# Seven half products for pairs of gate slots in the last FFN of a two-layer decoder step

## The reference, cut to what matters

```python
def swiglu(x, w_gate, w_up, w_down):
    h = jax.nn.silu(jnp.einsum('bsd,df->bsf', x, w_gate)) * jnp.einsum('bsd,df->bsf', x, w_up)
    return jnp.einsum('bsf,fd->bsd', h, w_down)
...
    x = x + rms_norm(swiglu(h, w_ffn_gate[i], w_ffn_up[i], w_ffn_down[i]), g_post_ffn[i])
```

## Time and profile before

| | |
|---|---|
| median of 3 runs | 2570.3 us (2569.86 to 2570.42) |
| span of the profiled execution | 2568.3 us |
| the profiled execution's own time | not listed beside its span; the median is 2.0 us over the span |
| PE / DVE / ACT busy | 2555.7 / 1501.2 / 1011.8 us |
| mean granted clock of PE | 0.999 |

### The profile page before, as it was taken

One profiled execution on the slowest core, in us unless ns is written; L12 is line 12 of the kernel. 1 busy time (PEld: TensorE's weight loads), 2 busy tenths in 40 slices (PEclk: granted clock), 3 DMA queues, 4 the chain that ended last, 5 costly groups with the idle time before them and its releaser, 6 DMA issues.

```text
span 2568.3 us, 40710 instructions
## 1 busy us (share of the span) xinstructions
PE 2555.7 (100%) x17201; PEld 2315.5 (90%) x17201; DVE 1501.2 (58%) x2320; ACT 1011.8 (39%) x1452; POOL 0.2 (0%) x4
## 2 busy tenths in 40 slices
PE   9999999999999999999999999999999999999998
PEld 7899898887988998899999988998887989999998
DVE  6644575666466673357854775328876486434435
ACT  5443355452344443345434444335552343222222
POOL 0000000000000000000000000000000000000000
PEclk9999999999999999999999999999999999999999
DMA  6454445445433433553333343444346334322222
GB/s 226 136 184 154 138 159 159 140 119 163 148 113 107 135 100 97 169 161 95 112 108 103 103 147 117 139 147 127 108 130 202 115 115 139 104 83 85 87 84 91
DMA packets 176704, 330.38 MB, mean 129 GB/s; under 512 B 19964, under 2 KB 93436, under 8 KB 176524
## 3 DMA queue, kind: packets, MB, share of 16 engines
q1 hardware_dynamic: 176524, 327.79, 40.9%
HBM read 271.46 MB, written 56.28 MB: 128 GB/s over the span
## 4 chain that ended last, share of the span: by engine, by line
PE 93%; DVE 4%; ACT 2%; issue 1%; DMA 0%; SPq 0%; ACTq 0%; DVEq 0%
PE ps L1016 81%; PE ps L1030 3%; PE ps L1342 1%; PE ps L1284 1%; PE ps L1428 1%; DVE Y L1886 1%; PE ps L1273 1%; PE ps L1267 1%; PE ps L1146 0%; DVE w_lo L1815 0%; PE ps L1048 0%; PE ps L1266 0%; PE ps L1375 0%; PE ps L1379 0%; PE ps L1376 0%
## 5 line engine op out<-in xcount | busy, mean ns | idle before, releaser
L1016 PE MATMUL ps<-HH,w_lo 128*128 128x288 f32 (+1 forms) x3480 | 1137.8, 327 | 0.2 <-DVE w_lo L1815 0.2
L1016 PE MATMUL ps<-HL,w_hi 128*128 128x288 f32 (+1 forms) x3480 | 1128.1, 324 | 0.0
L1016 PE MATMUL ps<-HH,w_hi 128*128 128x288 f32 (+1 forms) x3480 | 1127.4, 324 | 0.0
L1016 PEld LDWEIGHTS ps<-HH,w_lo 128*128 128x128 f32 x3480 | 652.9, 188 | 48.7 <-issue 5.8
L1016 PEld LDWEIGHTS ps<-HL,w_hi 128*128 128x128 f32 x3480 | 652.8, 188 | 42.9
L1016 PEld LDWEIGHTS ps<-HH,w_hi 128*128 128x128 f32 x3480 | 653.0, 188 | 41.7
L1815 DVE TENSOR_TENSOR w_lo<-w_stage,w_hi 128x1024 fp32r<-128x1024 f32 x392 | 478.7, 1221 | 253.6 <-ACT w_hi L1462 252.5
L1462 ACT ACTIVATE w_hi<-w_stage 128x1024 fp32r<-128x1024 f32 x392 | 412.1, 1051 | 333.4 <-PE ps L1016 302.7
L1016 PE MATMUL ps<-hid_hi,w_lo 128*128 128x288 f32 (+1 forms) x1052 | 347.8, 331 | 1.7 <-DVE Y L1886 1.1
L1016 PE MATMUL ps<-hid_lo,w_hi 128*128 128x288 f32 (+1 forms) x1052 | 343.5, 327 | 0.0
L1016 PE MATMUL ps<-hid_hi,w_hi 128*128 128x288 f32 (+1 forms) x1052 | 343.3, 326 | 0.0
(11 more groups left out here) (270 smaller groups left out, 1886.1 us busy)
## 6 DMA issues: line engine op xcount, KB each, us to landing
w_stage<-w_gate_in SPq DMA_DIRECT2D x88, 512.0 KB, 3.7
w_stage<-w_up_in SPq DMA_DIRECT2D x88, 512.0 KB, 3.6
w_stage<-w_down_in SPq DMA_DIRECT2D x88, 512.0 KB, 3.6
w_stage<-w_in_in SPq DMA_DIRECT2D x80, 512.0 KB, 3.8
w_stage<-w_out_in SPq DMA_DIRECT2D x32, 512.0 KB, 3.8
proj_scratch<-evicted SPq DMA_DIRECT2D x48, 288.0 KB, 2.2
proj_scratch<-evicted SPq DMA_DIRECT2D x32, 256.0 KB, 2.1
w_stage<-w_v_in SPq DMA_DIRECT2D x16, 512.0 KB, 4.2
```

The costliest lines, as they stand in the source:

```text
L1016: mm = pe.matmul(ps[:, grp.bank + t, 0:W], wsl(w, k), x[:, k, t * W:(t + 1) * W], start=(k == first and m == 0), stop=(k == last and m == 2))
```

## The change

**The products.** For b = 0 to 8 the gate units 2b+2 and 2b+3 stand side by side and are one 2x2 product: two output tiles (slots a and b), two halves of the inner dimension (512 each), two halves of the tokens (288 each). Eight half products of 12 matmuls become seven, by Strassen's scheme in Winograd's form. It needs sums of weight halves (S1 to S4, 128x512 each) and of quarters of the normalised block (T, 4 x 288 columns each), all split into high and low halves, and sums of products (U2, U3, C22, C21, C12, 128x288 each). The other units keep their whole products; the order becomes `G(2b+2) G(2b+3) D(b,0) D(b,1) U(2b+2) U(2b+3)`. The tenth pair keeps the old order.

**Where it stands.** DVE makes S3 and S2 at the end of the step two units ahead of a pair, and S1, low S2, S4, low S1 at the end of the step one unit ahead, which is that of U(2b+1). The T quarters are summed in place in `n.xs` (two in each of the two steps ahead of G(0)) and split in the steps of G(0), U(0) and G(1). Norm 7 writes its result in place for this, the load of x for norm 8 moves behind the last split, and norm 8's tiles move from the first units of B1 to the second gate unit of pairs 1 to 8, one tile each. The load into the first slot of a pair waits for S4 too.

```diff
@@ Plan.ffn
+            if layer == 1 and blk == 1 and b < PAIRS - 2:
+                out += self.seven(Seven(b, "G"), U, 2 * b + 2)
+                out += [U("D", b, 0), U("D", b, 1), U("U", 2 * b + 2), U("U", 2 * b + 3)]
+                continue
@@ Plan.banks
+                if not u.second:
+                    z.banks = [(at + c) % 4 for c in range(3)]
+                    z.vacated = [dict([held[b]]) for b in z.banks]
+                    at = (at + 3) % 4
...
+                    held[z.banks[0]] = ("act", z.c11)
+                    held[z.banks[1]] = ("dve", z.c21)
+                    held[z.banks[2]] = ("dve", z.c12)
@@ schedule
-    tag(u - 1, "xload", 8)
-    ffn_norm(3, 0, u + 1, ((1, 2), (2, 1), (5, 2), (6, 3)))
+    f = at["G", 1, 1, 0, 0]
+    for i in range(4):
+        tag(f - 2 + i // 2, "tsum", i)
+        tag(f + (0, 0, 3, 4)[i], "tq", i)
+    tag(f + 5, "xload", 8)
+    ffn_norm(3, 0, u + 1, [(at["G", 1, 1, 2 * p + 1, 0] - u - 1, 1) for p in range(2, 10)])
@@ SP: load
+                if n - NW in sevens:
+                    sp.wait_ge(s["sums"], 4 * (sevens[n - NW].g + 1))
@@ PE
+            def half_product(hi, lo, xh, xl, bank, start=True):
+                for k in range(KD // 2):
+                    for m, (w, x) in enumerate(((lo, xh), (hi, xh), (hi, xl))):
+                        mm = pe.matmul(ps[:, bank, 0:GW[1]], w[:, k * P:(k + 1) * P], x[:, k, :],
...
+            def seven_first(z):
...
+                vacant(z.vacated[0])
+                half_product(g.whi[:, a, 0:512], g.wlo[:, a, 0:512], quarter(HH, 0, 0), quarter(HL, 0, 0), X).then_inc(s["prod"], 1)
+                pe.wait_ge(s["s_lo"], 3 * z.g + 1)
+                if z.g == 0:
+                    pe.wait_ge(s["t_lo"], 4)
+                vacant(z.vacated[1])
+                half_product(g.S2H, g.S2L, g.TH[:, 2], g.TL[:, 2], Y).then_inc(s["prod"], 1)
+                pe.wait_ge(s["s_lo"], 3 * z.g + 2)
+                vacant(z.vacated[2])
+                half_product(g.S1H, g.S1L, g.TH[:, 0], g.TL[:, 0], Z).then_inc(s["prod"], 1)
+                pe.wait_ge(s["w_lo"], z.n + 2)
+                pe.wait_ge(s["left_dve"], z.u2)
+                half_product(g.whi[:, b, 0:512], g.wlo[:, b, 0:512], g.TH[:, 1], g.TL[:, 1], Y, False
+                             ).then_inc(s["prod"], 1)
+            def seven_second(z):
...
+                pe.wait_ge(s["left_act"], z.t1)
+                half_product(... slot a, second half, quarter(HH, 1, 0) ..., X, False).then_inc(s["groups"], 1)
+                pe.wait_ge(s["left_dve"], z.u3)
+                half_product(... slot b, second half, g.TH[:, 3], g.TL[:, 3], Y).then_inc(s["groups"], 1)
+                pe.wait_ge(s["s_lo"], 3 * z.g + 3)
+                pe.wait_ge(s["left_dve"], z.c22)
+                half_product(g.S4H, g.S4L, quarter(HH, 1, 1), quarter(HL, 1, 1), Z, False).then_inc(s["prod"], 1)
@@ ACT
+            def seven_unit(n, u):
+                z = u.seven
+                if not u.second:
+                    s4_high(z)
+                    hi(n + 2)
+                    first_copy(z)
+                    return
+                first_silu(u)
+                hi(n + 2)
+                second_silu(z)
...
                 if n + 2 < len(units):
                     hi(n + 2)
+                between(n)
...
                 evict(u)
+                if n + 1 in sevens:
+                    s2_s1_high(sevens[n + 1])
@@ DVE
+            def seven_first(n, z):
+                s_low(z, 2)
+                u2_sum(z)
+                lo(n + 2)
+            def seven_second(n, z):
+                u3_c22(z)
+                lo(n + 2)
+                c21(z)
+            def seven_ahead(n):
+                if n + 2 in sevens:
+                    s3_s2(sevens[n + 2])
+                if n + 1 in sevens:
+                    z = sevens[n + 1]
+                    s1_sum(z)
+                    s_low(z, 0)
+                    s4_sum(z)
+                    s_low(z, 1)
...
+                if ended(n):
+                    c12(ended(n))
                 if u.kind != "D" and n + 2 < len(units):
                     lo(n + 2)
...
                     if t[0] in steps and t[:2] != ("rstd", 0) and t != plan.middle(u):
                         steps[t[0]](*t[1:])
+                seven_ahead(n)
```

More of the change, by code:

```diff
@@ L63, in __init__ @@
         self.tags = []
+        self.seven, self.second = None, False
         self.late = kind == "P" and layer == 0 and blk == 0
@@ L150, in banks @@
         for u in self.units:
+            if u.seven:
+                z = u.seven
[3 more added lines that the diff above has]
+                    at = (at + 3) % 4
+                    z.t1 = counts["act"] = counts["act"] + 1
+                    z.u2 = counts["dve"] = counts["dve"] + 1
+                else:
+                    order = ("u3", "c22", "c21", "c12")
+                    z.c11 = counts["act"] = counts["act"] + 1
+                    ev = {}
+                    for name in order:
+                        counts["dve"] += 1
+                        ev[name] = counts["dve"]
+                    z.u3, z.c22, z.c21, z.c12 = ev["u3"], ev["c22"], ev["c21"], ev["c12"]
+                    held[z.banks[0]] = ("act", z.c11)
+                    held[z.banks[1]] = ("dve", z.c21)
+                    held[z.banks[2]] = ("dve", z.c12)
+                u.groups.append(Group(n, z.banks[u.second], {}, 0))
+                n += 1
+                continue
             by = "dve" if u.kind in "UD" or u.late else "act"
@@ L564 @@
     "half_small", "outs", "y_stored",
+    "sums", "s_hi", "s_lo", "t_sum", "t_hi", "t_lo", "prod", "silu",
 )
@@ L578, in program, with normed @@
     BY_ROWS = ((0, 0), (32, 0))
+    def normed(N, k):
+        return g.n.xs[:, k, 0:NT[1]] if N.n == 7 else g.n.t[:, k % 2, 0:NT[N.blk]]
     PIECE = lambda st: (st // 4, (0, 2, 1, 3)[st % 4])
@@ L677, in unit, with ended, quarter @@
         return units[plan.at[kind, layer, blk, i, j]]
+    sevens = {}
+    for n, u in enumerate(units):
+        if u.seven and not u.second:
+            sevens[n] = u.seven
+            u.seven.n, u.seven.hid0 = n, u.hid0
+    def ended(n):
+        return units[n - 1].seven if n and units[n - 1].second else None
+    def quarter(ap, k, t):
+        return ap[:, 4 * k:4 * k + 4, t * GW[1]:(t + 1) * GW[1]]
+    T_PLACE = ((0, 0), (0, 1), (1, 1), (1, 0))
+    U3 = lambda: g.E[:, 2, 0:GW[1]]
+    U2 = lambda: g.E[:, 2, GW[1]:NT[1]]
     gained = 0
@@ L1087, in dense @@
                     return
+                if u.seven:
+                    seven_first(u.seven) if not u.second else seven_second(u.seven)
+                    return
                 pe.wait_ge(s["w_lo"], n + 1)
@@ L1458, in hi @@
                 u = units[n]
+                if u.second:
+                    act.wait_ge(s["sums"], 4 * u.seven.g + 1)
                 if u.narrow:
@@ new lines, in first_copy, with first_silu @@
+            def first_copy(z):
+                act.wait_ge(s["prod"], 5 * z.g + 1)
+                act.wait_ge(s["hid_lo_ready"], z.hid0)
+                act.activation(U3(), ps[:, z.banks[0], 0:GW[1]], ACT.Copy).then_inc(s["left_act"], 1)
+            def first_silu(u):
+                z = u.seven
+                act.wait_ge(s["groups"], units[z.n].groups[0].n + 1)
+                act.wait_ge(s["hid_lo_ready"], z.hid0)
+                act.activation(g.E[:, 0, 0:GW[1]], ps[:, z.banks[0], 0:GW[1]], ACT.Silu).then_inc(s["left_act"], 1)
+                table["now"] = "silu"
@@ L1471, in evict, with between, t_half @@
+            def between(n):
+                if ended(n):
+                    third_silu(ended(n))
+            def t_half(i):
+                act.wait_ge(s["t_sum"], 4)
+                if i == 0:
+                    act.wait_ge(s["groups"], unit("U", 1, 0, KF - 1).groups[-1].n + 1)
+                act.activation(g.TH[:, i], quarter(g.n.xs, *T_PLACE[i]), ACT.Copy).then_inc(s["t_hi"], 1)
             def evict(u):
@@ new lines, in add_to, with u2_sum, u3_c22 @@
+            def add_to(out, bank, u):
+                return dve.tensor_tensor(out, ps[:, bank, 0:GW[1]], u, ALU.add).then_inc(s["left_dve"], 1)
+            def u2_sum(z):
+                dve.wait_ge(s["prod"], 5 * z.g + 2)
+                dve.wait_ge(s["left_act"], z.t1)
+                dve.wait_ge(s["hid_lo_ready"], z.hid0)
+                add_to(U2(), z.banks[1], U3())
+            def u3_c22(z):
+                dve.wait_ge(s["prod"], 5 * z.g + 4)
+                add_to(U3(), z.banks[1], U3())
+                dve.wait_ge(s["left_dve"], z.u3)
+                add_to(g.E[:, 1, GW[1]:], z.banks[2], U3())
@@ L1865, in evict @@
                     dve.wait_ge(s["groups"], grp.n + 1)
-                    dve.wait_ge(s["left_act"], unit("G", u.layer, b, u.i).groups[0].ev)
+                    gate = unit("G", u.layer, b, u.i)
+                    if gate.seven:
+                        dve.wait_ge(s["left_act"], gate.seven.c11)
```

(11 more changed lines are left out.)

132 lines of the change are left out of this document (124 added, 8 removed).

## The result

The changed kernel takes 2594.55 us in the median (2593.09 to 2595.80, 4 runs), the kernel before 2570.24 in the same runs: 1.0093 times as long, interval 1.0079 to 1.0107. It is slower by 24.3 us. The forecast was 2581.9 with a range of 2574 to 2590: the direction was right, the size was about half.

The account below looks back on a forecast made before the run. PE alone was taken to bound the kernel. Terms -14.3 + 20.3 + 2.2 + 3.2 + 0.15 = +11.6 us took the span from 2568.3 to 2579.9, so 2581.9 us was forecast, range 2574 to 2590.

Parts of the forecast that it names:

- Matmuls removed: Nine gate pairs on PE: 84 matmuls instead of 96 each, 1.59 us saved a pair, -14.3 us in all.
- The wait for low S2: Product 2 of each pair: PE waits 2.15 us for DVE, 2.25 with the new start, +20.3 us; first pair 0.15 more.
- Product 4: Fourth half product of a pair: its operand U2 was to be ready 0.15 us before PE asks, so no wait.
- rival B: Product 2's operands are there in time, so the change is faster: 2561.5 us, chance 0.05.
- Down units: Down units behind each pair: PE waits for late C21 and C12 on DVE, 0.25 us a pair, +2.2 us.
- The head: Start of the last FFN: T's sums and splits make DVE's evictions late, U(0) starts 3.2 us later.
- The clock: PE's granted clock during the pairs' waits: stays full, so no cost in the forecast.
- Rival D: Clock falls in each pair's wait, two products at half rate, 3.2 us a pair, 29 in all: 2611 us, chance 0.04.
- A: The forecast itself: product 2 waits in every pair; own range 2576 to 2587 us, chance 0.76.

Follow-up runs that it names:

- late_nine: Changed kernel with sums and copies reordered on DVE and ACT, T's sums and splits later, norm 8's tiles moved, pairs b = 1 to 9; 2558.49 us, ratio 0.9950.
- sums_first: Changed kernel with a pair's sums and splits ahead of the eviction of U(2b+1) on DVE and ACT; 2572.28 us, ratio 1.0006.
- head_only: Changed kernel with all nine pairs back to whole products in the old order, T's sums and splits and the norm changes kept; 2574.25 us, ratio 1.0014.
- filled: Changed kernel with product 1 done again into a spare PSUM bank, 12 more matmuls in each pair's wait; 2584.48 us, ratio 1.0054.
- half_filled: Changed kernel with 6 more matmuls per pair into a spare bank, the first half of product 1 again; 2584.25 us, ratio 1.0050.

## Why the prediction was right in the direction and half in the size

**Matmuls removed, -14.3:** right; 108 fewer, and in late_nine the pairs keep 9 x 1.37 = 12.3 of it.

**The wait for low S2, +20.3 and 0.15 for the first pair:** right in place, cause and size: 2.15 us and a new start in eight pairs, 2.47 in the first, 20.6 in all. sums_first removes it by the order alone. The reading of the queue held too: the idle 39% of DVE were no help, since the sums could not start before an eviction that PE itself released.

**Product 4, in time by 0.15:** this did not quite hold. U2 was done 0.1 later than forecast, and in the pair without a fall product 4 came 0.13 late with its new start; in the others the clock's fall hid it. When the wait in front went, it came to 0.8 us a pair. The prediction priced rival B as if only one wait stood between the change and its gain. sums_first at 2572.3 shows two: at 2561.5 rival B was 11 us too good.

**Down units, +2.2:** 2.7 by the 192 matmuls. Right in place; before the first group PE lost 0.13 and not 0.04.

**The head, +3.2:** 3.3 in the profile, 3.5 in head_only. DVE's late eviction starts at 2129.41; 2128.5 was forecast, with 0.67 of the difference already there ahead of the change.

**The clock, nothing:** this is the step that failed. The prediction read that the clock fell 2.4 us after PE had stopped for good, saw its own 2.15 just below, and took the row as a bound: "the wait is shorter than the idleness that the end shows", chance 0.04. One fall seen gives no such bound. Rival D was what happened, beside A and not in place of it, and its price was too high: 3.2 us a pair in all nine, against 1.50 in seven or eight. filled and half_filled show the cause: more matmuls in the wait, less time. In spans, 25.4 - 11.6 = 13.8 us were missing: 12.0 for the clock, 0.7 ahead of the change, 0.5 at the down units, 0.3 for the first pair's longer wait and product 4, 0.1 in the head; the rest is unassigned. The 0.7 is there from the start of the program: the unit that starts at 18.52 us in the kernel before starts at 19.22 here and at 19.70 in the second profile of the same kernel. It varies between executions, and no run shows it to be the change's doing.

**The cases:** D was a mechanism that adds to A, but stood in the list as its alternative. The range, cut at 2590, left out A with D.

## What to carry to other kernels

A sum that saves work on the bounding engine has to be written into the helper's in-order queue where its inputs are ready, not where the code is convenient: here the same kinds of sums and splits, placed elsewhere in the queues and for nine pairs that leave out the first, turned +24 us into -12. When a wait goes, compute the next thing's due time again without it, on all queues, before naming the gain. And price an idle gap on TensorE like the one here, about two microseconds, with the clock's fall behind it; if the gap can't go, try a few throwaway matmuls in it: here 6 were enough and took 10 us off.

## What the runs showed of the hardware

The granted clock fell after 15 of 18 waits (two profiles of the changed kernel): after 14 of 16 of 2.15 us, and after one of two of 2.47 us. In the pair looked at above it fell while PE was at work again, about a microsecond after its return, and came back by itself; 14 matmuls started 0.24 us apart, 1.50 us lost. After the nine waits of half_filled (eight of 1.36 us, one of 1.68) and the nine for U2 in sums_first (eight of 0.81 us, one of 1.36) it stayed full. What lies between 1.68 and 2.15 us no run shows. Two executions of the same program thus differed by one fall. The Trainium skill, "TensorE: Matmul & The Clock Gate" (section "Why this matters for your kernels"), warns of idle gaps between bursts; these traces agree in kind. The gap that the page warns of is longer than the 2.15 us that were enough here, and the measurement decides.
